# Five products per k tile instead of six in the z, r, x and s units of a hybrid decoder layer

## The reference, cut to what matters

```
h = rmsnorm(x, g_pre) * (1 + scale) + shift
q, k, v, z_a, z_b, xbc, dt, r_a, r_b = split(h @ w_in)
o_a = dilated_attention(q, k, v, caches) * silu(z_a)      # prompt and decode
xs, B, C = split(silu(causal_conv(xbc)))
y   = rmsnorm(ssd(xs, dt, B, C, state) * silu(z_b))
out = (sigmoid(r_a) * (o_a @ w_o_a) + sigmoid(r_b) * (y @ w_o_b)) @ w_o
y_out = x + gate * rmsnorm(out, g_post)
```

## Time and profile before

| | |
|---|---|
| median of 3 runs | 3034.97 us (3028.29, 3036.03, 3034.97) |
| profiled execution | 3028.3 us, its span 3026.5 us |
| TensorE clock granted, mean | 0.997 |
| PE busy | 2973.9 us, 98% of the span |
| DVE / ACT / POOL busy | 62% / 29% / 40% |

### The profile page before, as it was taken

How to read it: one execution, slowest core, us unless ns; L and a number is a source line. 1 busy time by engine, 2 the same in 40 slices (tenths; PEclk the granted TensorE clock), 3 DMA queues, 4 the chain that set the end, 5 groups by cost and what they waited for, 6 DMA issues and landing times.

```text
span 3026.5 us, 52526 instructions
## 1 busy us (share of the span) xinstructions
PE 2973.9 (98%) x22660; PEld 2835.5 (94%) x22660; DVE 1867.1 (62%) x2044; ACT 867.3 (29%) x1239; POOL 1213.2 (40%) x576
## 2 busy tenths in 40 slices
PE   6999999999999999999999999999999999999998
PEld 4898999999999999999999999999999989999886
DVE  3303688888785787878887756766668665211302
ACT  3111222333233223233222242333323343211312
POOL 1133444433333333334444544444444434444332
PEclk9999999999999999999999999999999999999999
DMA  8878786554446786647567666656556666876643
GB/s 335 327 272 320 313 302 242 211 204 128 148 141 212 268 286 236 205 172 259 228 249 251 244 229 214 235 197 238 209 201 236 228 204 213 291 255 250 251 174 139
DMA packets 220460, 704.86 MB, mean 233 GB/s; under 512 B 26739, under 2 KB 129899, under 8 KB 170795
## 3 DMA queue, kind: packets, MB, share of 16 engines
q1 hardware_dynamic: 157686, 471.33, 44.7%
q0 software_dynamic: 5248, 174.60, 14.2%
q10 hardware_dynamic: 57296, 55.59, 5.5%
HBM read 630.85 MB, written 245.17 MB: 289 GB/s over the span
## 4 chain that ended last, share of the span: by engine, by line
PE 95%; DMA 2%; DVE 1%; SPq 0%; issue 0%; ACT 0%; POOL 0%; DVEq 0%; POOLq 0%; ACTq 0%
PE acc L1374 25%; PE acc L1376 25%; PE acc L1375 25%; PE ps_s L1247 2%; PE ps_s L1528 1%; PE ps_s L1413 1%; PE ps_w L1433 1%; PE ps_s L1494 1%; PE ps_t L1388 1%; PE ps_s L1421 1%; PE ps_s L1613 1%; PE ps_s L1612 1%; PE ps_s L1614 1%; DMA w_raw<-in_w_ada_t 1%; PE ps_s L1515 0%; PE ps_s L1414 0%
## 5 line engine op out<-in xcount | busy, mean ns | idle before, releaser
L893 POOL TENSOR_TENSOR w_lo<-w_raw,w_hi 128x1024 fp32r<-128x1024 f32 (+1 forms) x416 | 1074.5, 2601 | 1765.7 <-ACT w_hi L944 1765.7
L1374 PE MATMUL acc<-act,w_hi 128*128 128x288 f32 x5744 | 1718.3, 299 | 1.8 <-POOL w_lo L893 1.8
L1376 PE MATMUL acc<-act,w_lo 128*128 128x288 f32 x5744 | 1691.9, 295 | 0.0
L1375 PE MATMUL acc<-act,w_hi 128*128 128x288 f32 x5744 | 1691.8, 295 | 0.0
L1374 PEld LDWEIGHTS acc<-act,w_hi 128*128 128x128 f32 x5744 | 1078.2, 188 | 26.1 <-issue 21.9
L1375 PEld LDWEIGHTS acc<-act,w_hi 128*128 128x128 f32 x5744 | 1078.6, 188 | 1.1
L1376 PEld LDWEIGHTS acc<-act,w_lo 128*128 128x128 f32 x5744 | 1077.7, 188 | 0.0
L944 ACT ACTIVATE w_hi<-w_raw 128x1024 fp32r<-128x1024 f32 (+1 forms) x418 | 403.8, 1015 | 475.3 <-PE acc L1376 192.6
L1814 DVE TENSOR_TENSOR side<-side 128x2048 f32<-128x2048 f32 x96 | 282.3, 2941 | 98.0 <-DMA side<-in_vals_t 85.3
L1012 ACT ACTIVATE ev<-acc 128x576 f32<-128x576 f32 x144 | 93.7, 651 | 823.7 <-PE acc L1376 820.3
L1785 DVE TENSOR_TENSOR side<-side 128x2048 f32<-128x2048 f32 x96 | 269.1, 2803 | 84.7 <-DMA side<-in_keys_t 82.0
(11 more groups left out here) (331 smaller groups left out, 2741.0 us busy)
## 6 DMA issues: line engine op xcount, KB each, us to landing
w_raw<-in_w_in_t SPq DMA_DIRECT2D x160, 1024.0 KB, 7.5
out_s_kv<-in_cache_a_w POOLq DMA_DIRECT2D x80, 1632.0 KB, 9.0
side<-in_keys_t SPq DMA_DIRECT2D x52, 1024.0 KB, 8.1
side<-in_vals_t SPq DMA_DIRECT2D x52, 1024.0 KB, 8.0
w_raw<-in_w_ada_t SPq DMA_DIRECT2D x40, 1024.0 KB, 7.7
out_s_kv<-in_cache_a_w POOLq DMA_DIRECT2D x24, 1344.0 KB, 7.9
w_raw<-in_w_o_b_t SPq DMA_DIRECT2D x16, 1024.0 KB, 7.2
w_raw<-in_w_o_t SPq DMA_DIRECT2D x16, 1024.0 KB, 8.6
```

The lines of the kernel that those rows point to most:

```text
L893: nc.gpsimd.tensor_tensor(dst, raw[:, SLOT[s], ks, 0:cols], wh[:, u % 2, ks, 0:cols].bitcast(F32), ALU.subtract).then_inc(lo, 1)
L1374: nc.tensor.matmul(out, wh[:, c, k, 0:cols], high, start=(k == 0), stop=False)
L1375: nc.tensor.matmul(out, wh[:, c, k, 0:cols], low, start=False, stop=False)
L1376: mm = nc.tensor.matmul(out, wl[:, c, k, 0:cols], high, start=False, stop=(k == kt - 1))
```

## The change

In the units of kind r, s, x and z (88 units: 8 z, 32 r, 32 x, 16 s; `PAIRED`) the tokens are no longer cut in 288 + 288 but in 256 + 320. The first bank takes in columns 0 to 255 the low sums wh·hL of tokens 0 to 255 and in columns 256 to 511 their high sums wh·hH + wl·hH. One product with 512 moving columns, the low limb's 256 beside the high limb's 256, makes wh·hL and wh·hH together, and a second one of 256 columns adds wl·hH (`front`). The second bank takes tokens 256 to 575 with three products of 320 columns as before (`back`). A k tile so takes five products with 512 + 256 + 3 × 320 = 1728 columns, where it took six with 6 × 288 = 1728.

The two parts of the first bank must be added. After the unit ACT copies the low sums (128 x 256) from PSUM to SBUF (`store_low`, in the place of `store_unit`). DVE adds them to the high sums in PSUM (`fold_low`, at the very start of half 2(u + 1), before all else of that half). After `high(u + 2)` ACT copies the 576 sums out, now a contiguous row over both banks (`store_sums`), and raises `evac`.

```diff
+FRONT = 256
+PAIRED = [kind in "rsxz" and u >= 2 for u, kind in enumerate(KINDS)]
+FOLDS = [sum(PAIRED[:u + 1]) for u in range(NU)]
...
+        def limbs(k):
+            return act[:, k:2 * KT:KT, 0:FRONT]
+        def sums(u):
+            n = FRONT if PAIRED[u] else HALF
+            return acc[u % 2][0:unit_cols(u)[1], :, :].rearrange("p a n -> p (a n)")[:, 512 - n:512 - n + TOK]
...
+            def store_low(u):
+                act_e.wait_ge(used, u + 1)
...
+                nc.scalar.activation(front_home(u), low_sums(u), ACT.Copy).then_inc(low_out, 1)
+            def store_sums(u):
+                c, (col, cols) = u % 2, unit_cols(u)
+                kind, g, n = UNITS[u]
+                act_e.wait_ge(folded, FOLDS[u])
+                func = {"s": ACT.Silu, "z": ACT.Silu, "r": ACT.Sigmoid}.get(kind, ACT.Copy)
+                out = zs[:, n, :] if kind == "s" else ev[:, c, :]
+                nc.scalar.activation(out, sums(u), func).then_inc(evac, 1)
...
-                if KINDS[u] not in "ABO":
+                if PAIRED[u]:
+                    store_low(u)
+                elif KINDS[u] not in "ABO":
                     store_unit(u)
...
                     high(u + 2)
+                if PAIRED[u]:
+                    store_sums(u)
...
+            def front(u, k):
+                c, both = u % 2, acc[u % 2][:, 0, :].rearrange("p (a n) -> p a n", a=2)
+                nc.tensor.matmul(both, wh[:, c, k, :], limbs(k)[:, ::-1, :], start=(k == 0), stop=False)
+                mm = nc.tensor.matmul(high_sums(u), wl[:, c, k, :], hH[:, k, 0:FRONT], start=False, stop=(k == KT - 1))
+                return mm
+            def back(u, k):
+                c, out = u % 2, acc[u % 2][:, 1, 0:TOK - FRONT]
+                nc.tensor.matmul(out, wh[:, c, k, :], hH[:, k, FRONT:TOK], start=(k == 0), stop=False)
+                nc.tensor.matmul(out, wh[:, c, k, :], hL[:, k, FRONT:TOK], start=False, stop=False)
+                return nc.tensor.matmul(out, wl[:, c, k, :], hH[:, k, FRONT:TOK], start=False, stop=(k == KT - 1))
...
+            def fold_low(u):
+                dve.wait_ge(low_out, FOLDS[u])
+                TT(high_sums(u), high_sums(u), front_home(u), ALU.add).then_inc(folded, 1)
...
             for half in range(2 * NU):
                 u = half // 2
                 if half % 2 == 0 and u:
+                    if PAIRED[u - 1]:
+                        fold_low(u - 1)
```

27 lines of the change are left out of this document (26 added, 1 removed).

## The result

| | before | changed |
|---|---|---|
| median | 3033.7 us | 3058.4 us (3056.7 to 3059.9) |
| ratio to before | | 1.0084, 95% interval 1.0066 to 1.0101 |
| profiled execution, span | 3026.5 us | 3056.7 us |
| granted clock, mean | 0.997 | 0.994 |

What follows compares the result with a forecast made beforehand. PE, busy 98% of the span, was taken to bound the kernel. The terms -18.7 + 12.9 + 1.5 + 2.5 + 1.7 = -0.1 us gave a forecast of 3035 us (3026 to 3044); the range leaving out 2 in 10 was 3018 to 3050.

Steps and rivals of the forecast that it cites:

- The saving, 18.7 us: PE's products in 88 units: one in six goes, each saving a fixed 13.3 ns, 0.213 us per unit, 18.7 us in all.
- The break, taken at nothing: The 512-column product's moving operand lies in two pieces; its one break was costed at nothing, with 18 us kept for the range.
- Rival B: The operand's break costs time in all 1408 512-column products; 10 ns each would give +14, 3049 us; chance 0.10.
- Rival C: No fixed part is saved, five products take as long as six: 3035 + 18.7 = 3054 us; chance 0.04.
- Units 98 to 105, 12.9 us: DVE reaches its folds late, so PE loses 12.9 us: 2.9 at unit 100, the other 10 at unit 105.
- The 2.9 us at unit 100: PE's stop at unit 100, because DVE's fold of unit 98 comes 27.2 us after unit 97's end; 2.9 us.
- The clock, 1.5 us: After the 10 us stop of PE at unit 105 the clock falls to the 1.2 GHz level, costing 1.5 us.
- Units 85 to 90, 2.5 us: ACT's transposed-weight copy and exponent stand behind `store_sums` and stop PE, with smaller pieces at 85 and 89; 2.5 us (1 to 5).
- Unit 161, 1.7 us: ACT's split starts later, behind `store_low`, a table load and `store_sums`, so PE starts 1.7 us later.
- Units 111 to 160 at nothing: State-space units: the fold fits DVE's gap and ACT's later steps aren't needed yet; no cost, else up to a microsecond per unit.
- Slower: Chance 0.19 that the change measures slower than the forecast by more than 0.3%, 9.1 us.
- Rival D: Waits spread to z units 65 and 30 and more r units, plus a second low-clock stretch: +8, 3043 us; chance 0.10.

## Why the prediction was wrong, step by step

**The saving, 18.7 us: mis-sized, it was about 5** (the run without the addition, -4.9). The step that failed is "one product in six goes. By the fixed part that is 13.3 ns x 16 k tiles = 0.213 us per unit". A fixed part read from two rows was taken to hold everywhere. The earlier trace rows show the slower half of a unit; the other runs at 131.6 ns. And the pair of 512 and 256 columns takes 353 ns, not 347. Both errors are a few ns, but each stands 16 times in a unit against a saving of 13 ns: 0.09 us (6.40 - 6.31) and 0.10 us (5.65 - 5.55) of 0.21 in 62 units; in the other 26 only the first stands. The 320 and the 256 columns were right (147 and 113 to 120 against 147 and 120). The 2.5 ns of the Trainium skill's page TensorE: Matmul & The Clock Gate, section Back-to-back issue gap, are further off still: 320 + 2 x 2.5 would be 325 ns a pair, an estimate from that page, and the traces have 346 to 353. That the 3.5 us of saving by that page came nearer to the 4.9 measured than 18.7 did is luck, since no interval fits it.

**The break, taken at nothing: right.** Rival B gave the right order of the time, 3049, by a mechanism that the run with one piece refutes. Rival C, no saving, came nearest in the number with 3054 and in the products was three quarters right; but its reason, that the fixed part isn't there, is refuted by the second half and by the 26 units, and its time held none of the stops that make the loss. The interval of 235 ns alone looked like a break; only the run without it told.

**Units 98 to 105, 12.9 us: the place and the chain right, the size 6.2.** The 2.9 us at unit 100 didn't come. The fold of unit 98 ran 23.5 us after unit 97's end (taken as in the sum at ACT's first instruction behind it, 1550.21), not 27.2, and the copy-out ended 0.5 us before PE asked. It was close: in the second trace of the changed kernel PE waited 0.1 us there, and 0.5 in the run with the moved addition.


```profile
1550.21 0.39 ACT L1025 ACTIVATE ev<-acc 128x256 f32<-128x256 f32 x1 [9.80 <-PE acc L1409]
...
1573.74 0.42 DVE L2190 TENSOR_TENSOR acc<-acc,ev 128x256 f32<-128x256 f32 x1
...
1551.70 4.92 POOL L917 TENSOR_TENSOR w_lo<-w_raw,w_hi 128x1024 fp32r<-128x1024 f32 x2 [6.04 <-ACT w_hi L968]
```

The last values are sent when GpSimd's pair ends, and that took 4.92 us here and 6.83 in the earlier trace rows. I had taken 6.83 as a property of the pair. It hangs on which engine comes first: before, a multiplication of DVE (1549.56) ran ahead of GpSimd's second instruction; here that instruction was first and DVE's multiplication took 4.22 us (at 1554.55) where 2.29 is usual. The addition of unit 103 came 93.7 us after unit 97's end, against the 99.3 in the sum (98.2 + 1.6 - 0.5), while units of 12.69 us and not 12.51 had PE ask 1.2 us later: 12.9 less 5.6 and 1.2 is the 6.2 measured, to 0.1.

**The clock, 1.5 us: about right there** (1.3, the step at unit 106, and 2.8 in the second trace), but there were more of them: behind unit 116 in both traces. The one at unit 177 isn't in the second trace, and the run without the addition has one there too, so it is not the change's. The mean granted clock is 0.994 against 0.997.

**Units 85 to 90, 2.5 us: about right.** The steps at units 87 to 89 add up to 2.1.

**Unit 161, 1.7 us: right in place and cause**, it was 2.94 - 1.24 = 1.7 in idle time, 2.4 in the start of the unit.

**Units 111 to 160 at nothing: this failed, by 14 us** (9.1 at unit 116, 4.9 behind it). The prediction looked at one unit with slack and said of ACT's steps that they "are needed 5 us later". It named the exposure, up to a microsecond a unit, and then didn't look for the chains. Both have to do with GpSimd's pair, which the prediction gave no price. DVE's convolution ahead of unit 116 stands beside the pair already in the trace of before; one addition waits for 4 us of held instructions, and an unrelated SiLU waits for the addition. And in six groups the chain from L1155 had 2.0 us to spare, which were lost because a step of 0.5 us between DVE and GpSimd put GpSimd first (2.70 us for 0.88). "`store_low` is shorter than the 0.65 us that it replaces" was taken as harmless; it is half of that step.

**The chances.** Slower had 0.19, and the range ended at 3050. Rival D (the waits spread, +8) came nearest in its mechanism, with a third of the price and without the state space. The sum had ended near nothing only because an over-sized saving (18.7 for 5) stood against stops and clock of which 18.6 were counted and some 30 came.

## What to carry to other kernels

When a change trades a few ns in each of thousands of instructions, read the present cost in every phase (both halves, each stretch of the program), not from one row; and try the order of the instructions as well as their number. When it puts a step of a lightly used engine between PE and its next unit, walk through all places of that engine's in-order list and ask at each how late it is there: 62% busy left 21 to 24 us of stops and low clock. An earlier start can cost as much as a later one, where two engines hold each other. A consumer that must hand back PSUM should not stand behind work that is late for its own reasons; where it must, one moved instruction or one added wait elsewhere may be worth more than the edit.
